# Moving the decay distances of a gated linear attention into the input projection, and giving both level multiplies to GpSimd

## The reference

```python
def gla_chunked(q, k, v, log_a):                 # chunks of 64 positions, 4 heads of 64 key channels
    causal = jnp.tril(jnp.ones((C, C), bool))[:, :, None]
    def step(S, inp):
        q_c, k_c, v_c, a_c = inp
        b = jnp.cumsum(a_c, axis=-2)
        diff = b[..., :, None, :] - b[..., None, :, :]
        dec = jnp.exp(jnp.where(causal, diff, -jnp.inf))
        attn = jnp.einsum('bhid,bhjd,bhijd->bhij', q_c, k_c, dec)
        o = (jnp.einsum('bhid,bhde->bhie', q_c * jnp.exp(b), S)
             + jnp.einsum('bhij,bhje->bhie', attn, v_c))
        b_last = b[..., -1:, :]
        S = (jnp.exp(b_last)[..., 0, :, None] * S
             + jnp.einsum('bhjd,bhje->bhde', k_c * jnp.exp(b_last - b), v_c))
        return S, o
...
    n = rmsnorm(h, g_mix[i])
    proj = n @ w_in[i]
    gq, gk, gv, gr, glr, dqkv, dz, da, db = jnp.split(proj, split_idx, axis=-1)
    log_a = jax.nn.log_sigmoid((glr @ w_gla_gate[i] + b_gla_gate[i]).astype(jnp.float32)) / GLA_GATE_NORM
    o_gla = gla_chunked(...)
    o_gla = rmsnorm(from_chunks(o_gla), g_gla_out[i]).reshape(B, S, GLA_WIDTH) * jax.nn.silu(gr)
    qkv = jax.nn.silu(causal_dwconv(dqkv, w_conv[i]))
...
```

## Time and profile before

| | |
|---|---|
| Time, median of 3 executions | 2489.5 us (2487.5 to 2493.74) |
| Profiled execution, its own time | 2487.37 us |
| Span of the profiled execution | 2485.6 us, 48175 instructions |
| Granted TensorE clock, mean over the span | 0.978 |
| Busy: PE / DVE / ACT / POOL | 97% / 46% / 23% / 13% |
| Input projection | about 0 to 378 us |
| GLA stage, of which steps 2 to 13 | about 378 to 473 us; 387.7 to 426.4 us |

### The profile page before, as it was taken

The page is one execution under the profiler, slowest core; times in us unless marked ns, Lnnn a source line. Parts: engine busy times, 40 slices in busy tenths (PEclk is TensorE's granted clock), DMA queues, the critical chain, the costliest instruction groups (busy, mean ns, idle before and its releaser), DMA issues. The chain is left out here.

```text
span 2485.6 us, 48175 instructions
## 1 busy us (share of the span) xinstructions
PE 2406.5 (97%) x19229; PEld 2175.7 (88%) x19230; DVE 1141.2 (46%) x1928; ACT 567.5 (23%) x1199; POOL 328.1 (13%) x345
## 2 busy tenths in 40 slices
PE   8999999989897999999999999999999999999898
PEld 6787787687444999999999999999999999999776
DVE  4666718675225333333343343444433434343495
ACT  4434424553111001111111111111111111111265
POOL 0000116162001000001100110110101001010230
PEclk9999997999998999999999999999999999999899
DMA  4111211001613766677788888888898988888562
GB/s 153 43 50 48 89 60 44 27 3 32 258 68 132 249 228 229 245 255 268 276 299 289 282 302 313 302 315 319 312 324 311 321 310 315 322 307 318 200 208 77
DMA packets 113980, 528.46 MB, mean 213 GB/s; under 512 B 15044, under 2 KB 38808, under 8 KB 64696
## 3 DMA queue, kind: packets, MB, share of 16 engines
q1 hardware_dynamic: 99160, 481.16, 54.3%
q0 software_dynamic: 14688, 45.37, 5.6%
HBM read 485.84 MB, written 40.63 MB: 212 GB/s over the span
## 5 line engine op out<-in xcount | busy, mean ns | idle before, releaser
L1865 PE MATMUL ex_psum<-ex_xT,weight_ring_a 128*128 128x134 f32 (+14 forms) x7168 | 901.1, 287 | 3.8 <-DVE ex_xT L1850 3.7
L1865 PEld LDWEIGHTS ex_psum<-ex_xT,weight_ring_a 128*128 128x128 f32 x7168 | 886.5, 191 | 5.5 <-issue 4.8
L1907 PE MATMUL ex_psum<-ex_hT,weight_ring_b 128*128 128x134 f32 (+14 forms) x4096 | 506.0, 286 | 0.0
L1907 PEld LDWEIGHTS ex_psum<-ex_hT,weight_ring_b 128*128 128x128 f32 x4096 | 503.0, 191 | 0.0
L1726 POOL DMA_INDIRECT ex_rows<-xn_dram,ex_list x170 | 162.5, 956 | 1372.7 <-DVE ex_list L1769 1322.3
L1875 DVE TENSOR_SCALAR ex_gate<-ex_psum,bias_gate_up 128x192 f32<-128x192 f32 x256 | 92.6, 403 | 524.0 <-PE ex_psum L1865 515.5
L1879 DVE TENSOR_SCALAR ex_up<-ex_psum,bias_gate_up 128x192 f32<-128x192 f32 x256 | 94.9, 412 | 388.4 <-PE ex_psum L1865 230.2
L1892 ACT ACTIVATE ex_sig<-ex_gate 128x384 f32<-128x384 f32 x128 | 66.9, 523 | 767.5 <-DVE ex_gate L1875 736.5
L1917 ACT ACTIVATE ex_yT<-ex_psum,bias_down 128x192 f32<-128x192 f32 x256 | 83.3, 437 | 500.8 <-PE ex_psum L1907 500.8
L2168 PE MATMUL project_psum<-n_hi,w_in_hi 128*128 128x512 f32 x464 | 187.4, 404 | 2.9 <-DVE n_lo L520 2.9
L2168 PE MATMUL project_psum<-n_lo,w_in_hi 128*128 128x512 f32 x464 | 182.2, 393 | 0.0
(11 more groups left out here) (344 smaller groups left out, 2420.6 us busy)
## 6 DMA issues: line engine op xcount, KB each, us to landing
weight_ring_a<-in_w_gate_up SPq DMA_DIRECT2D x224, 1024.0 KB, 5.4
weight_ring_b<-in_w_down SPq DMA_DIRECT2D x128, 1024.0 KB, 7.0
weight_ring_b<-in_w_gate_up SPq DMA_DIRECT2D x32, 1024.0 KB, 7.2
y_dram<-ex_y SPq DMA_DIRECT2D x80, 192.0 KB, 6.1
w_in_pieces<-in_w_in SPq DMA_DIRECT2D x29, 512.0 KB, 3.5
y_dram<-ex_y SPq DMA_DIRECT2D x52, 128.0 KB, 5.6
project_work<-in_x SPq DMA_DIRECT2D x8, 512.0 KB, 7.3
gates_dram<-project_work POOLq DMA_DIRECT2D x16, 256.0 KB, 2.9
```

What stands on the lines that cost most here:

```text
L1865: mm = pe.matmul(self.ps[:, bank, i * CAP:i * CAP + width], w[:, k, i * P:(i + 1) * P], self.xT[:, k, 0:width], start=(k == 0), stop=(k == ...
L1907: mm = pe.matmul(self.ps[:, bank, first:first + width], w[:, i, j], self.hT[:, k, 0:width], start=(k == 0 and j % 2 == 0), stop=(k == KT - ...
```

## The change

Four things change.

1. In the projection GpSimd makes all 12 tiles of distances, both halves (24 `tensor_tensor` of 128x512), right after `run_sum`. It builds them in the two `qkvT` tiles that the last two convolution blocks will fill (j = 10, 11), and stores each with a DMA of 512 KB to a new DRAM tensor `dist_dram`. VectorE waits for the stores (`dist_all`) before it writes block 10.
2. In the GLA stage SP loads the tiles back into a ring of four `dist` buffers: steps 2 to 5 first, then `gv`, then each further tile once its buffer is free (four steps later), then the gates.
3. GpSimd makes Q and K of every step, one after the other. VectorE keeps only the masked copies.
4. The two masked copies of a step become one over both PSUM banks; it starts when both banks are written.

```diff
@@ project: gpsimd @@
             pool.memset(g.gqkT[:, 0, 0:P + HALF], 0.0).then_inc(blank, 1)
+            pool.wait_ge(run_sum, 2)
+            for n, (level, p) in enumerate(LEVEL_STEPS):
+                at = g.qkvT[:, NQKV - 2 + n % 2, :]
+                if n >= 2:
+                    pool.wait_ge(dist_out[n % 2], 16 * (n // 2))
+                first, second = block_halves(at, level)
+                b_first, b_second = block_halves(g.b[:, p, :], level)
+                middle = block_middle(g.b[:, p, :], level)
+                pool.tensor_tensor(first, middle, b_first, ALU.subtract).then_inc(dist_made, 1)
+                pool.tensor_tensor(second, b_second, middle, ALU.subtract).then_inc(dist_made, 1)
+                pool.wait_ge(dist_made, 2 * n + 2)
+                pool.dma_start(g.dist_dram[n], at).then_inc(dist_out[n % 2], 16)
+            for s in dist_out:
+                pool.wait_ge(s, 16 * len(LEVEL_STEPS) // 2).then_inc(dist_all, 1)
@@ project: vector @@
                 dve.wait_ge(sig_done, j + 1)
+                if j == NQKV - 2:
+                    dve.wait_ge(dist_all, 2)
                 dve.tensor_tensor(g.qkvT[:, j, :], acc[j % 2], sg, ALU.mult).then_inc(silu_done, 1)
@@ gla: sync @@
-            sp.dma_start(g.gv[:], g.gv_dram.rearrange("(t p) d -> p t d", p=P)).then_inc(gv_in, 16)
+            for n in range(2, len(STEPS)):
+                if n >= 2 + DISTS:
+                    sp.wait_ge(q_done, n - 1 - DISTS)
+                    sp.wait_ge(k_done, n - 1 - DISTS)
+                sp.dma_start(dist[:, n % DISTS, :], g.dist_dram[n - 2]).then_inc(dist_in[n % DISTS], 16)
+                if n == 1 + DISTS:
+                    sp.dma_start(g.gv[:], g.gv_dram.rearrange("(t p) d -> p t d", p=P)).then_inc(gv_in, 16)
@@ gla: gpsimd @@
-            k_distance(2)
             pool.memset(A[:], 0.0).then_inc(zeroed, 1)
-            k_distance(3)
             for n in range(2, len(STEPS)):
...
-                pool.tensor_tensor(halves(K[:, n % 2, :], level)[0], halves(g.gqkT[:, 2 + p, :], level)[0], halves(dist[:, n % 2, :], level)[0],
-                                   ALU.mult).then_inc(k_done, 1)
-                if n + 2 < len(STEPS):
-                    k_distance(n + 2)
+                pool.tensor_tensor(block_halves(Q[:, n % 2, :], level)[1], block_halves(g.gqkT[:, p, :], level)[1],
+                                   block_halves(dist[:, n % DISTS, :], level)[1], ALU.mult).then_inc(q_done, 1)
+                pool.tensor_tensor(block_halves(K[:, n % 2, :], level)[0], block_halves(g.gqkT[:, 2 + p, :], level)[0],
+                                   block_halves(dist[:, n % DISTS, :], level)[0], ALU.mult).then_inc(k_done, 1)
@@ gla: scalar @@
-                act.wait_ge(q_dist, n - 1)
-                act.wait_ge(k_dist, n - 1)
-                act.activation(dist[:, n % 2, :], dist[:, n % 2, :], ACT.Exp, scale=1.0 / 16).then_inc(decay_done, 1)
+                act.wait_ge(dist_in[n % DISTS], 16 * ((n - 2) // DISTS + 1))
+                act.activation(dist[:, n % DISTS, :], dist[:, n % DISTS, :], ACT.Exp, scale=1.0 / 16).then_inc(decay_done, 1)
@@ gla: vector (q_distance and q_level are gone) @@
-                for parity in range(2):
-                    dve.wait_ge(score_done, 2 * n + parity + 1)
-                    dve.copy_predicated(A[:, 2 * p + parity], mask.bitcast(I32).unsqueeze(1).to_broadcast([P, NT, C]),
-                                        ps[:, bank_of(n, parity), :].rearrange("p (t c) -> p t c", t=NT)).then_inc(kept, 1)
+                dve.wait_ge(score_done, 2 * n + 2)
+                if n >= 2:
+                    dve.wait_ge(kept, 2 * (n - 1))
+                dve.copy_predicated(A[:, 2 * p:2 * p + 2].rearrange("p a t c -> p (a t) c"), mask.bitcast(I32).unsqueeze(1).to_broadcast([P, 2 * NT, C]),
+                                    ps[:, bank_of(n, 0):bank_of(n, 1) + 1, :].rearrange("p a (t c) -> p (a t) c", t=NT)).then_inc(kept, 2)
...
             for n in range(len(STEPS)):
                 keep(n)
-                if n + 2 < len(STEPS):
-                    q_level(n + 2)
-                if n + 4 < len(STEPS):
-                    q_distance(n + 4)
```

More of the change, by code:

```diff
@@ L169, in project @@
         sq_done, ss_done, l2_root, l2_inv, l2_done = (sem(n) for n in ("l2_squares", "l2_sums", "l2_root", "l2_inverse", "l2_done"))
+        dist_made, dist_out, dist_all = sem("distances"), [sem(f"distances_out{i}") for i in range(2)], sem("distances_stored")
         gate_sig, rows_out = sem("gate_sigmoid"), [sem(f"rows_out{i}") for i in range(2)]
@@ L653, in w_in_pieces, with block_halves, block_middle @@
     return np.ascontiguousarray(np.concatenate(cols, axis=1).reshape(KT, P, -1, P).transpose(2, 1, 0, 3).reshape(-1, P, D))
+LEVEL_STEPS = [(l, p) for l in range(LEVELS) for p in range(2)]
+def block_halves(ap, level):
+    m = 1 << level
+    v = ap.rearrange("p (a i) -> p a i", i=2 * m)
+    return v[:, :, 0:m], v[:, :, m:2 * m]
+def block_middle(ap, level):
+    m = 1 << level
+    return ap.rearrange("p (a i) -> p a i", i=2 * m)[:, :, m - 1:m].to_broadcast([P, T // (2 * m), m])
 def gla(nc, g, sem):
-    STEPS = [("diag", p) for p in range(2)] + [(l, p) for l in range(LEVELS) for p in range(2)]
+    STEPS = [("diag", p) for p in range(2)] + LEVEL_STEPS
+    DISTS = 4
     with ExitStack() as ph:
@@ L672, in gla @@
         cut = sb("gla_level_masks", [P, 1 + LEVELS, C])
-        dist = sb("gla_dist", [P, 2, T])
+        dist = sb("gla_dist", [P, DISTS, T])
         Q = sb("gla_q_level", [P, 2, T])
@@ L687, in gla @@
         rest_zeroed, blanked = sem("rest_zeroed"), sem("level_rows_zeroed")
-        masks_done, q_dist, k_dist = sem("level_masks"), sem("q_distance"), sem("k_distance")
+        masks_done, dist_in = sem("level_masks"), [sem(f"distances_in{i}") for i in range(DISTS)]
         score_done, kept = sem("scores"), sem("scores_kept")
@@ L699, in bank_of @@
             return 2 * (step % 4) + parity
-        def halves(ap, level):
-            m = 1 << level
-            v = ap.rearrange("p (a i) -> p a i", i=2 * m)
-            return v[:, :, 0:m], v[:, :, m:2 * m]
-        def middle(level, p):
-            m = 1 << level
-            return b[:, p, :].rearrange("p (a i) -> p a i", i=2 * m)[:, :, m - 1:m].to_broadcast([P, T // (2 * m), m])
         @block.sync
         def _(sp):
-            sp.dma_start(g.gv[:], g.gv_dram.rearrange("(t p) d -> p t d", p=P)).then_inc(gv_in, 16)
+            for n in range(2, len(STEPS)):
[5 more added lines that the diff above has]
+                    sp.dma_start(g.gv[:], g.gv_dram.rearrange("(t p) d -> p t d", p=P)).then_inc(gv_in, 16)
             for t in range(NT):
@@ L722, in _ @@
         def _(pool):
-            def k_distance(n):
-                level, p = STEPS[n]
-                if n >= 4:
-                    pool.wait_ge(q_done, n - 3)
-                    pool.wait_ge(k_done, n - 3)
-                pool.tensor_tensor(halves(dist[:, n % 2, :], level)[0], middle(level, p), halves(b[:, p, :], level)[0], ALU.subtract).then_inc(k_dist, 1)
-            k_distance(2)
             pool.memset(A[:], 0.0).then_inc(zeroed, 1)
-            k_distance(3)
             for n in range(2, len(STEPS)):
@@ L2509, in program @@
     g.gates_dram = nc.dram_tensor("gates_dram", (2, T, HALF), F32).ap()
+    g.dist_dram = nc.dram_tensor("distances_dram", (len(LEVEL_STEPS), P, T), F32).ap()
     g.gv_dram = nc.dram_tensor("gv_dram", (T, HALF), F32).ap()
```

17 lines of the change are left out of this document (removed).

## The result

| | before | after |
|---|---|---|
| median of 20 runs each, us | 2488.65 (2486.43 to 2494.17) | 2493.41 (2489.64 to 2497.35) |
| ratio of times, 95% interval | | 1.0015 [1.0009, 1.0022], that is +3.7 us [+2.2, +5.5] |
| profiled execution, us | 2487.37, span 2485.6 | 2493.97, span 2492.1 |
| mean granted clock of TensorE | 0.978 | 0.974 |
| GLA stage begins (diagonal matmuls) | 378.08 | 382.76 |

A gain of 1.0 was forecast and a loss is clear of the noise. The table places it: the input projection ends 4.7 us later (0.5 of that stands there already at 81 us, before the first distance is made), and the GLA stage then takes 92.3 us instead of 94.7. So the stage that the change is about did more than was forecast, and the stage in which "TensorE does not wait" was forecast pays it all back.

A forecast was written before the change was run, and what follows sets the result against it. TensorE, 97% busy, was taken as the bound, with VectorE holding GLA steps 2 to 13. Start +1.8, steps -3.4, tail +0.65 and projection 0 gave about -1.0: 2486.4 us profiled, 2488.5 median, range 2483 to 2494.5.

The forecast's parts named there:

- TensorE does not wait: Input projection: VectorE's delay from GpSimd's subtractions stays within what is allowed, so TensorE loses 0.
- The projection, 0: Term for the input projection: 24 GpSimd subtractions delay VectorE by 21 us in all, adding 0 to the time.
- VectorE 1.76, or 35% of the time: Projection: each distance tile costs VectorE 1.76 us, two subtractions at 0.88, which is 35% of the time.
- a tile ... near 5 us: Projection: one distance tile takes GpSimd 2 x (1.04 + 0.9) + 0.8 + 0.2, near 5 us; 12 tiles take 60.
- TensorE waits for VectorE only through the low parts of the weights: Projection: the low parts are the only link; VectorE may be delayed 6.7 us until block 4's, 10.6 until block 5's.
- lag reaches TensorE: Rival, chance 0.1: in the projection VectorE loses 57% of its time and TensorE stands 10.5 us; 2498.0.
- The 25 us allowed by 150: Projection: VectorE loses 21 us over the 12 tiles, and by 150 us a delay of 25 is allowed.
- The start, +1.8: Start of the GLA stage: step 2 waits for a distance load from DRAM; its matmuls start at 389.46, 1.8 us later.
- Steps 2 to 13 with the start: -1.6: GLA levels: GpSimd bounds steps 2 to 5, then TensorE at 2.92 a step; they end at 424.8, 1.6 us earlier.
- the tail +0.65: After the GLA levels: the merged masked copy starts at the same signal but takes all of 1.34, +0.65 us.
- The loads land together: Rival, chance 0.1: at the GLA start the first of four loads lands with the fourth, 5.5 us later; 2493.0.
- the clock holds: Rival, chance 0.2: TensorE's clock stays 1.00 through the GLA levels and GpSimd bounds every step; -4.7 us, 2484.8.

The follow-up runs named there:

- p3: The changed kernel with VectorE making the low part of a block's weights ahead of the taps instead of behind them; 2496.13 us, ratio 1.0031 to the kernel before.
- p1: The kernel before, with the distances made and stored in the projection as in the change but not read by the GLA stage; 2493.47 us, ratio 1.0022.
- r1: The changed kernel measured once more, without an edit; 2492.25 us, ratio 1.001 to the kernel before.
- c3: The paced kernel with one 384-column filling matmul behind each of steps 2 to 12 and a three-step PSUM ring; 2485.26 us, ratio 0.9989 to the kernel before.
- the paced kernel: The changed kernel with GpSimd's distance tiles spread out, two per convolution block from block 3 on; 2489.73 us, ratio 1.0004 to the kernel before.
- c4: As c3, but with a filling matmul of 192 columns instead of 384; 2489.14 us, ratio 0.9995 to the kernel before.

## Why the prediction was wrong

- **The projection, 0, measured +4.2: here the forecast failed.** The failing step is "VectorE 1.76, or 35% of the time", with "a tile ... near 5 us" under it. The loss per subtraction was right (0.88 forecast, 0.84 measured; 21 in all, measured 20.2). But GpSimd waits less than I took: mostly only the second subtraction of a tile waits, and in five tiles of 12 that one by 0.5 or less. A tile takes 3.89, the loss is 44%, and the same 20 us fall into 46 us instead of 60.
- **The step behind it was not carried through.** I checked block 4 and block 5 and then the total at 150 us. Block 6 decides. Up to its low part VectorE has 20.9 us of work: at 44% that is +16.4 (measured 135.56 against 118.43 before, +16.6 when the 0.5 of the start is taken off), where about 14.5 are allowed. At the 35% of the forecast it is +11.3, and fits. A sum over blocks with the rate left open would have shown that the margin ends at 41% (20.9 us of work in 35.4), six points above the forecast.
- **A second link was overlooked.** "TensorE waits for VectorE only through the low parts of the weights" is false: ScalarE's copy out of PSUM stands in its queue behind the sigmoid, which waits for the taps. In this kernel that link cost nothing: the copy ended at 135.26, and the group that needs it would have begun at 138.7 even without the pause. In p3, where it ended at 140.25, it stopped TensorE for 3.17.
- **The pause's clock cost was overlooked.** The rival priced the pause alone; 2.4 of pause brought 1.7 of slow matmuls here and in p1 and r1. In p3 pauses of 3.17 and 3.00 brought none, so the price is not certain.
- **The rival "lag reaches TensorE"** was the right mechanism at less than a quarter of its price: 2.4 of pause for 10.5, since GpSimd neither waited each time nor never. The price was also summed wrongly: at a loss of 57% the 13.9 us of work up to block 5's low part lose 18.4, not all 21.1, which leaves a pause of 7.8. And 2498.0, like the 2493.0 of the late loads, takes the -1.0 off twice; by their own terms they are 2499.0 and 2494.0. The 25 us allowed by 150 is not in the sum over blocks either (18.4 for block 7, 22.3 for block 8). None of this moves the forecast.
- **The start, +1.8, measured 0.** The load landed earlier (3.2 from issue to exp, with the table load already done, instead of 5.3), which leaves the `keep_running` matmuls as the bound, as before.
- **Steps 2 to 13 with the start: -1.6 forecast, -2.7 measured; the tail +0.65, measured +0.6 at the recurrence's first output matmul and +0.3 at the stage's end.** TensorE at 0.50 is the bound, as forecast, at 3.05 a step instead of 2.92 (5.89 for two and a gap of 0.21, where I had taken 5.83 and none). The clock fell only in step 4, so the first three took 2.75 to 2.93.
- **"The loads land together"** did not happen; **"the clock holds"** did not happen in the changed kernel, and in c3 it was worth 4.0 within the levels; c3's whole time, the other gains of the paced kernel included, is 2.7 [0.5, 5.0] below the kernel before.

The forecast number lay 4.9 below the measured median; that the measured one is inside the range is luck: the range reaches up to 2494.5 for late loads and the spread of the runs, and neither put it there.

## What to carry to other kernels

When work is put on GpSimd beside a VectorE that feeds the bounding engine, count not only the total that VectorE loses but where it stands at each hand-over, with the rate as an unknown, and ask for each block which rate makes it late. If the total fits, spread the work (one wait per tile removed the whole pause here, 4.2 us of the stage) rather than reorder the delayed engine: the low part moved ahead cured its own hand-over and made the next one late, 5.4 us behind it. When a row names a releaser that ended well before the wait did, read in the kernel which semaphores that instruction waits for. And price a pause of TensorE with its clock: 1.7 us in three profiles here, nothing in one.

## What the runs showed of the hardware

- **Two-input operations on VectorE and GpSimd shut each other out, unevenly.** In a dense stream of both (the changed kernel) each VectorE operation grew by 0.8 to 1.2, about the length of one GpSimd subtraction, while of GpSimd's second subtractions seven in twelve grew by 1.0 to 1.2 and the first ones hardly. The first tap, with one tensor and a column of scalars, is caught too (0.75 to 1.53). GpSimd memsets of 0.5 cost the two-input operations nothing, but the first tap up to 0.4 (1.13 in p4).
- **One wider matmul in each step, and the clock held.** In the changed kernel 64x64 weight loads and matmuls that hardly pause stay at 0.50 to the end of the levels, as in the earlier trace rows; with one matmul of 192 or 384 columns in each step (c4, c3) the granted clock was 1.00 through the levels. The Trainium skill (TensorE: Matmul & The Clock Gate, section "Part 1: The HAM clock gate") says that activity releases it; for these 64x64 matmuls being busy alone did not.
- **A pause of 1.75 us sometimes costs the clock and sometimes doesn't**, in the same kernel and at the same place (9.6 us from the stage's start to step 2 in the first profile of the changed kernel, 12.8 in r1), and is then worth 3.2 to 4.8 us. In the projection pauses of 2.40 and 2.44 were followed by 0.50, pauses of 3.17 and 3.00 (p3) by 1.00.
